# Rows of the split activations placed 2112 and 2080 bytes apart, and three weight slots staggered by 32 and 64 bytes

## The reference, cut to what matters

```
x = x + 0.5 * (silu(rms(x) @ w_gate) * (rms(x) @ w_up)) @ w_down     # twice a layer; D_FF 2816, 2816, 2752
x = x + mixer(rms(x))   # layer 0: pooling and latent attention; 1: gated convolution; 2: Fourier mixing and attention
```

## Time and profile before

| what | value |
|---|---|
| median of three runs | 2834.17 us |
| profiled execution, and its span from first to last instruction | 2831.04 us, 2829.2 us |
| TensorE matmuls busy | 99% of the span, 12580 instructions |
| weight loads (beside the matmuls) busy | 80% |
| VectorE, ScalarE, GpSimd busy | 47%, 32%, 5% |
| mean granted TensorE clock | 0.997 of full speed |
| DMA | 30% of 16 engines, 90 GB/s |

### The profile page before, as it was taken

The page is one execution under the profiler, slowest core; times in us unless marked ns, Lnnn a source line. Parts: engine busy times, 40 slices in busy tenths (PEclk is TensorE's granted clock), DMA queues, the critical chain, the costliest instruction groups (busy, mean ns, idle before and its releaser), DMA issues.

```text
span 2829.2 us, 31389 instructions
## 1 busy us (share of the span) xinstructions
PE 2787.6 (99%) x12580; PEld 2261.9 (80%) x12580; DVE 1331.4 (47%) x1895; ACT 906.4 (32%) x1286; POOL 130.1 (5%) x130
## 2 busy tenths in 40 slices
PE   8999999999999999999999999999999999999998
PEld 7888878888888888888888888888877877788776
DVE  5444358654443344434554444334443557544433
ACT  4222226532222223222233222223222346422221
POOL 0000005300000000000000000000000114000000
PEclk9999999999999999999999999999999999999999
DMA  4332332033323332333323322333322320233222
GB/s 153 97 95 88 94 86 77 24 97 97 94 89 95 98 94 90 98 98 95 97 90 97 96 91 94 94 97 90 102 88 86 93 83 23 60 99 98 87 91 70
DMA packets 282704, 253.31 MB, mean 90 GB/s; under 512 B 8384, under 2 KB 278848, under 8 KB 282560
## 3 DMA queue, kind: packets, MB, share of 16 engines
q1 hardware_dynamic: 282560, 251.30, 29.5%
HBM read 249.17 MB, written 2.10 MB: 89 GB/s over the span
## 4 chain that ended last, share of the span: by engine, by line
PE 82%; issue 13%; DVE 3%; ACT 2%; DMA 0%; SPq 0%; POOLq 0%; POOL 0%; DVEq 0%
PE bank L382 28%; PE bank L384 27%; PE bank L383 26%; PE bank L471 1%; DVE a_mx L1237 0%; PE bank L435 0%; PE bank L424 0%; DVE wl L1128 0%; ACT Xh L806 0%; DVE a_nb L1144 0%; DMA raw<-in_ffn_w_gate 0%; ACT wh L775 0%; DVE a_KT L1140 0%; ACT a_P L859 0%; DVE X L1137 0%
## 5 line engine op out<-in xcount | busy, mean ns | idle before, releaser
L1128 DVE TENSOR_TENSOR wl<-raw,wh 128x1024 fp32r<-128x1024 f32 (+6 forms) x498 | 573.8, 1165 | 991.2 <-ACT wh L775 990.4
L382 PE MATMUL bank<-Xh,wl 128*128 128x512 f32 x2544 | 1016.1, 399 | 11.4 <-ACT Xh L806 8.4
L384 PE MATMUL bank<-Xh,wh 128*128 128x512 f32 x2544 | 998.1, 392 | 0.0
L383 PE MATMUL bank<-Xl,wh 128*128 128x512 f32 x2544 | 991.3, 390 | 0.0
L775 ACT ACTIVATE wh<-raw 128x1024 fp32r<-128x1024 f32 (+6 forms) x498 | 494.1, 1007 | 1018.5 <-PE bank L384 1013.3
L384 PEld LDWEIGHTS bank<-Xh,wh 128*128 128x128 f32 x2544 | 475.9, 187 | 123.4
L382 PEld LDWEIGHTS bank<-Xh,wl 128*128 128x128 f32 x2544 | 475.9, 187 | 119.3 <-issue 11.1
L383 PEld LDWEIGHTS bank<-Xl,wh 128*128 128x128 f32 x2544 | 476.7, 187 | 108.5 <-issue 1.9
L382 PE MATMUL bank<-Hh,wl 128*128 128x512 f32 x1056 | 421.2, 399 | 0.0
L384 PE MATMUL bank<-Hh,wh 128*128 128x512 f32 x1056 | 414.0, 392 | 0.0
L383 PE MATMUL bank<-Hl,wh 128*128 128x512 f32 x1056 | 410.9, 389 | 0.0
(11 more groups left out here) (264 smaller groups left out, 1579.8 us busy)
## 6 DMA issues: line engine op xcount, KB each, us to landing
raw<-in_ffn_w_gate SPq DMA_DIRECT2D x128, 512.0 KB, 3.7
raw<-in_ffn_w_up SPq DMA_DIRECT2D x128, 512.0 KB, 4.0
raw<-in_ffn_w_down SPq DMA_DIRECT2D x114, 512.0 KB, 3.4
raw<-in_c_w_in SPq DMA_DIRECT2D x24, 512.0 KB, 3.6
raw<-in_w_in SPq DMA_DIRECT2D x10, 512.0 KB, 3.7
raw<-in_a_w_in SPq DMA_DIRECT2D x8, 512.0 KB, 3.7
raw<-in_a_w_out SPq DMA_DIRECT2D x8, 512.0 KB, 3.3
raw<-in_c_w_out SPq DMA_DIRECT2D x8, 512.0 KB, 3.4
```

Source lines behind the costliest of these rows:

```text
L382: e.matmul(o, ll, rh, start=start, stop=False)
L383: e.matmul(o, lh, rl, start=False, stop=False)
L384: i = e.matmul(o, lh, rh, start=False, stop=stop)
L1128: e.tensor_tensor(lo, src, hi.bitcast(F), ALU.subtract).then_inc(wlo.up(("w", n)), 1)
```

## The change

Only places in SBUF change, no instruction. `sb` gets a second number, `off`: the tensor begins `off` bytes behind a multiple of `line`. `Xh` and `Xl` get 528 columns a row of which 512 are used, so their rows stand 2112 bytes apart (64 more than 2048). `Hh` and `Hl` get 520 columns a row, so theirs stand 2080 bytes apart (32 more). The slots 0, 1, 2 of `wh` begin 0, 32 and 64 bytes behind multiples of 2048, those of `wl` 0, 64 and 32 bytes behind. The `wl` slots now stand ahead of the `raw` buffers.

What moves with it: `raw` begins 64 bytes behind a multiple of 2048 (before 0), `par` 128 (before 64), and the mixers' tensors, whose rows stay 2048 bytes apart, begin 64 bytes behind a multiple (before 0). The engines' instructions stand in the same order with the same shapes and waits.

```diff
-        def sb(name, shape, dt, line=64):
+        def sb(name, shape, dt, line=64, off=0):
-            at = -(-place[0] // line) * line
+            at = -(-(place[0] - off) // line) * line + off
             place[0] = at + 4 * int(np.prod(shape[1:]))
...
         X = sb("X", [128, KT, T], F, 2048)
-        Xh = sb("Xh", [128, KT, T], R, 2048)
-        Xl = sb("Xl", [128, KT, T], R)
-        wh = [sb(f"wh{i}", [128, CAP], R, 2048) for i in range(N_RAW)]
+        Xh = sb("Xh", [128, KT, T + 16], R, 2048)[:, :, 0:T]
+        Xl = sb("Xl", [128, KT, T + 16], R, 2048)[:, :, 0:T]
+        wh = [sb(f"wh{i}", [128, CAP], R, 2048, off) for i, off in enumerate((0, 32, 64))]
+        wl = [sb(f"wl{i}", [128, CAP], R, 2048, off) for i, off in enumerate((0, 64, 32))]
         raw = [sb(f"raw{i}", [128, CAP], F) for i in range(N_RAW)]
         spare = sb("spare", [128, 1], F)
-        wl = [sb(f"wl{i}", [128, CAP], R) for i in range(N_RAW)]
...
-        H = [sb(n, [128, 22, T], R) for n in ("Hh", "Hl")]
+        H = [sb(n, [128, 22, T + 8], R, 2048)[:, :, 0:T] for n in ("Hh", "Hl")]
```

## The result

The changed kernel takes 2844.97 us (five runs, 2844.55 to 2847.39), the kernel before 2834.17 us in the same session. The ratio is 1.0041, with a 95% interval of 1.0027 to 1.0056: slower by 10.8 us, 0.4%. The profiled execution took 2844.55 us, span 2842.7, against 2831.04 and 2829.2.

A forecast was written before the change was run, and what follows sets the result against it. TensorE's matmul pace was taken as the bound. 10800 matmuls, each 1.1 ns quicker, gave -12 us, all else nothing: 2834.2 - 12 = 2822 us, with an 8 in 10 range of 2775 to 2850.

The forecast's parts named there:

- The bound and the leverage: TensorE's matmul pace alone bounds the kernel; each ns in the step of the 10800 affected matmuls is 10.8 us.
- The failed step: In mm3's 10800 matmuls, shifted rows break the settled pattern and quicken each step by 1.1 ns, -12 us.
- rows 5: Timeline stretch just after a TensorE stop: nine steps of the same operands in 2.07 us, 0.2300 each against the regular 0.2311.
- the settled order 236, 228, 229: Repeating step lengths in ns behind mm3's L382, L383 and L384, inferred from record lengths and a mean of 231.1.
- the slower rival: In mm3, the sweep meets more clashes than the settled pattern, behind L383 and L384: 2844 to 2862 us, chance 26%.
- the unchanged rival: In mm3, the pattern may come from matmul order and column count alone, so the time stays 2834 us; chance 19%.
- The change therefore doesn't pick one distance, it sweeps them: In mm3, row-to-tile distance takes multiples of 64 from 0 to 448 for X, of 32 up to 672 for H.
- The lower bound: Best case for the 10800 steps: about 226 ns kept up all the time, -4.6 ns each, -50 us.
- Nothing changes: Placement has no effect on TensorE, since loading the next tile steals no read bandwidth: 2834 us, chance 19%.

The follow-up runs named there:

- the cells of triples: Matmuls alone, not the full kernel: fp32r triples issued as in mm3, 512 combinations of row and tile addresses in steps of 32 bytes; 226.6 to 237.8 ns, mean 231.8.
- everything at 0: Kernel before, with the wl slots at multiples of 2048 too, so every streamed row and loaded tile stands at 0 modulo 256 bytes: 2786.84 us.
- the slots at 32: Rows at 0 and all wh and wl slots 32 bytes behind a multiple of 2048, against the kernel with all of these at 0: 2856.44 us.
- constant pairs: Matmuls alone, not the full kernel: 24 fp32r matmuls in a row with one streamed and one loaded address, 256 pairs; 226.7 ns at distance 0, 233 to 234 at most others.
- the kernel of distances: Matmuls alone, 512 columns: one row at 0 with tiles at several distances, then bf16, then walking rows; fp32r 226.7 ns at distance 0, 233.6 at 32.

## Why the prediction was wrong, point by point

- **The bound and the leverage: right.** TensorE's pace is all that moved. 10800 steps, 10.8 us for each ns, gives 12.6 us from the steps, and nothing came from raw, the splits or the waits.
- **The failed step** is the one that chose among the bounds: "I take rows 5 ... the settled order 236, 228, 229 needs every triple to look like the one before, which shifted rows deny it. That is -1.1 ns x 10800 = -12 us." The pattern did go, and the term had the wrong sign: +1.2 and +1.1 ns. I had taken the settled pattern for a bad one and disorder for a cure. At 231.1 it stood between the best, 226.7, and the mean over the cells of triples, 231.8; leaving it led to 232.2, near that mean. That the time lies within the range of 8 in 10 is owed to the slower rival's share of it: the forecast was 12 us faster, the result is 11 us slower.
- **The row under that step was read beyond its resolution, and at the wrong place.** 2.07 us in the earlier trace rows against 2.08 in the earlier trace rows is one unit of the timeline's rounding. By the finer start times both take 2080 ns, 231.1 a step: the ten matmuls of the earlier trace rows don't stand right behind the stop, and already have the settled pattern. So the earlier trace rows were neither a ground for a quicker pace nor, as the unchanged rival had it, for two paces at the same addresses. Nine steps soon behind the stop (from 29.89 to 31.96 us of the same trace) do have another pattern and take 2071 ns, 230.1 a step. The rounded numbers can't carry a sign of 1 ns, and three triples behind a stop say nothing of 10800 steps.
- **"The change therefore doesn't pick one distance, it sweeps them": right,** and the pace of a sweep was what the sum needed. No row of before shows one., 0.2320, from which the slower rival took 2844 us, isn't one either: the streamed slots stand at 0 and 64 there and the stationary tensor at 0, all the time. By start times that stage has 232.0 before, 226.9 with everything at 0 and 233.3 with the slots at 32. So that this rival, with a quarter of the chance, met the measured time to 1 us is luck in its number; its direction was right.
- **The rival's grounds were half wrong.** It said that wl loses its 64 bytes of distance in slot 0. The slots alone made the kernel faster by that very loss. What costs is that the rows walk through the distances, and it takes away all that the slots could gain: with walking rows the slots at 0, 32 and 64, all at 0, or before's gave 2845, 2843 and 2839.
- **The lower bound was right in size, not in cause.** -50 us for three steps of 226 was measured as -47 with everything at 0. I put it down to a shift that avoids a clash; it comes from no shift at all.
- **"Nothing changes" and the rule behind it.** The placement changes the pace by up to 6.6 ns a step, 70 us of this kernel. The Trainium skill ("TensorE: Matmul & The Clock Gate", Step-by-step: what each phase is for) says that loading the next tile "doesn't steal SBUF read bandwidth from the running matmul"; bf16 agrees, 216 at every distance; for fp32r the address of the loaded tile changes the pace of the running matmuls, from 226.7 to 233.7. That the two reads compete is not shown: tiles of 64 or 32 columns were slower at distance 0 and up to 4 ns quicker at 64 and 128.
- **What stays open** is the mechanism: why 256 bytes, why a distance of 4 bytes is worse than 16, why streamed addresses 16 off a multiple of 32 have another best distance, why a change of address from one matmul to the next costs, and by what history the same walk has two paces. The runs give the rule and the prices for constant addresses, and for the walks of this kernel, but no cause.

## What to carry to other kernels

Where TensorE streams fp32r back to back, put every streamed row and every loaded tile at the same address modulo 256 bytes, and that at 0 or another multiple of 32, in all slots and buffers, and keep row strides at multiples of 256; here, at 0, it was worth 1.65% with two lines (the other multiples of 32 were tried with matmuls alone). Staggering helped here only where it happened to bring a slot to distance 0; otherwise it trades a known pace for about the mean over all distances. Before taking 1 ns a step out of a timeline, compare it with the rounding, and count over hundreds of microseconds instead.

## What the runs showed of the hardware that I had not expected

- The step of a 512-column fp32r matmul depends on addresses modulo 256 bytes, from 226.7 to about 234 ns at constant pairs, in steady repetition; bf16 had 215.8 at all eight distances tried.
- The best distance depends on the streamed address: 226.7 ns at distance 0 where that address is a multiple of 32, 233.3 there for a row at 48.
- The same alternation of addresses, row and tile together at 0 and 128, ran at 236.6 ns in one kernel and at 228.4 in another, each steadily.
- At distance 0 a narrower tile was slower: 226.7, 229.3 and 231.8 ns for 128, 64 and 32 columns; at 64 and 128 it was as fast or faster.
- In the kernel of distances, with a tile of 64 columns at distance 0, 256, 384 and 512 streamed columns had 113.3, 173.3 and 230.0 ns: the first 128 more cost 60.0, the next 128 56.7, so the step is not proportional to the columns. At distance 32 they had 116.6, 175.0 and 231.6.
